# Expert stage of a two-model fp32 decoder kernel: extra places for weight chunks, filled at the stage's head

## What is computed

```python
h = h + hybrid_mixer(rms_norm(h, attn_norm[l]), ...)                     # model 1
h = h + hierarchical_moe(rms_norm(h, ffn_norm[l]), ...)
# model 2
x = x + gate1 * mixer(modulate(rms_norm(x, norm1_g), shift1, scale1))
x = x + gate2 * hier_moe(modulate(rms_norm(x, norm2_g), shift2, scale2), ...)
# every expert, for the tokens sent to it:
y = (silu(xb @ w_gate[e]) * (xb @ w_up[e])) @ w_down[e]
```

## Time and profile before

| | us |
|---|---|
| median of 3 runs | 2646.03 (2636.53 to 2647.21) |
| profiled execution, its time | 2646.7 |
| its span in the trace | 2644.5 |
| TensorE matmul busy | 2110.3 (80%) |
| VectorE busy | 631.6 (24%) |
| ScalarE busy | 361.4 (14%) |
| GpSimd busy | 59.7 (2%) |
| HBM read | 776.75 MB, 294 GB/s over the span |

### The profile page before, as it was taken

How to read it: one execution, slowest core, us unless ns; L and a number is a source line. 1 busy time by engine, 2 the same in 40 slices (tenths; PEclk the granted TensorE clock), 3 DMA queues, 4 the chain that set the end, 5 groups by cost and what they waited for, 6 DMA issues and landing times. The chain is left out here.

```text
span 2644.5 us, 33419 instructions
## 1 busy us (share of the span) xinstructions
PE 2110.3 (80%) x14160; PEld 1308.1 (49%) x14161; DVE 631.6 (24%) x1396; ACT 361.4 (14%) x733; POOL 59.7 (2%) x96
## 2 busy tenths in 40 slices
PE   7888779888777999899766666789999987666665
PEld 5564336564333688788422222238887862222222
DVE  4451104551012244453200000022441120000001
ACT  1520001520002131101100000011211020000000
POOL 0200000200000000000000000000000000000000
PEclk9999899999887999799888878799989988888888
DMA  9239999237998341386699999973302339999997
GB/s 385 120 145 427 428 428 399 95 139 309 429 428 357 112 159 66 129 344 239 273 428 429 428 428 429 428 291 128 132 31 96 127 128 423 427 429 428 429 428 306
DMA packets 55840, 779.33 MB, mean 295 GB/s; under 512 B 6840, under 2 KB 7096, under 8 KB 8120
## 3 DMA queue, kind: packets, MB, share of 16 engines
q1 hardware_dynamic: 55736, 777.82, 70.8%
HBM read 776.75 MB, written 1.05 MB: 294 GB/s over the span
## 5 line engine op out<-in xcount | busy, mean ns | idle before, releaser
L1899 PE MATMUL bank<-ring,arena 128*32 128x512 f32 x3136 | 505.5, 782 | 338.3 <-DMA ring<-in_w_exp 334.7
L1899 PEld LDWEIGHTS bank<-ring,arena 128*32 128x32 f32 x3136 | 102.2, 127 | 729.5 <-DMA ring<-in_w_exp 494.3
L1924 PE MATMUL bank<-ring,arena 128*32 128x512 f32 x1568 | 192.0, 628 | 66.5 <-DMA ring<-in_w_exp 43.8
L960 PE MATMUL bank<-xnT,ring 128*128 128x256 f32 x960 | 210.7, 379 | 0.0
L2079 DVE TENSOR_TENSOR arena<-bank,arena 128x256 f32<-128x256 f32 (+1 forms) x33 | 18.3, 554 | 795.7 <-PE bank L1899 566.4
L960 PEld LDWEIGHTS bank<-xnT,ring 128*128 128x128 f32 x960 | 181.6, 190 | 28.4 <-issue 4.5
L1636 PE MATMUL bank<-xnT,ring 128*128 128x256 f32 x768 | 177.2, 385 | 10.3 <-PEq L838 10.3
L1636 PEld LDWEIGHTS bank<-xnT,ring 128*128 128x128 f32 x768 | 148.3, 193 | 32.6 <-issue 11.9
L1869 PE MATMUL bank<-arena 128*128 128x256 f32 x592 | 144.6, 399 | 3.6 <-DVE arena L2090 3.6
L1869 PEld LDWEIGHTS bank<-arena 128*128 128x128 f32 x592 | 114.7, 200 | 65.0 <-issue 49.9
L1924 PEld LDWEIGHTS bank<-ring,arena 128*32 128x32 f32 x1568 | 50.2, 112 | 180.5 <-issue 95.2
(11 more groups left out here) (376 smaller groups left out, 2041.0 us busy)
## 6 DMA issues: line engine op xcount, KB each, us to landing
ring<-in_w_exp SPq DMA_DIRECT2D x288, 2048.0 KB, 25.7
arena<-in_w_ada SPq DMA_DIRECT2D x24, 2048.0 KB, 12.0
ring<-in_w_in SPq DMA_DIRECT2D x20, 2048.0 KB, 25.7
ring<-in_w_merge SPq DMA_DIRECT2D x18, 2048.0 KB, 7.9
ring<-in_w_o SPq DMA_DIRECT2D x8, 2048.0 KB, 10.3
ring<-in_w_conv SPq DMA_DIRECT2D x6, 2048.0 KB, 8.0
ring<-in_w_rest SPq DMA_DIRECT2D x2, 1696.0 KB, 25.5
small<-in_small SPq DMA_DIRECT2D x2, 1440.0 KB
```

The costliest lines, as they stand in the source:

```text
L960: last = nc.tensor.matmul(o[:, T * j:T * j + T], w[:, k, col:col + P], xnT[:, k, :], start=k == 0, stop=k == KT - 1)
L1899: last = nc.tensor.matmul(o[rows(e), :], Xw[:, k, rows(e)], ring[:, slot(n), at:at + MW], start=k == 0, stop=k == KT - 1)
L1924: last = nc.tensor.matmul(o[rows(e), :], hidT[:, j, rows(e)], ring[:, slot(n), at:at + MW], start=j == 0, stop=j == ft - 1)
```

## The change

Chunks that the ring has no slot for get places of their own in the arena, and are loaded during the head.

- `Xw` and `Yw` move from the arena into `xnT`; the rest of the stage's buffers move together, and the small scratch of e2's head moves into `small`. That leaves room for three chunks, `extra[0]` to `extra[2]`.
- e1 (`EXTRA1 = 2`): chunks 0 and 1 of quad 1 are loaded into `extra` at the head. GpSimd waits until the last item of quad 0 has used ring slots 0 and 1, and copies the two chunks there (128x4096 each), adding 16 to `w_loaded` as a load would. SyncE fetches quad 1 from chunk 2 on.
- e2 (`EXTRA2 = 3`): chunks 0 to 2 of quad 0 are loaded into `extra` at the head; the ring holds chunks 3 to 8 in place of 0 to 5. TensorE reads the first three from `extra` in item 0 and doesn't count them in `w_used`; SyncE fetches 9 to 11 as the ring frees.
- `extra[1]` overlies the scratch of the norm, so that its load waits for `scaled`. GpSimd's clearing of `Yw`, now in `xnT`, waits until the tokens are turned.

```diff
 RET, RWKV, LORA, CONV, MERGE, OUT2, MOE2 = 0, 4, 7, 8, 11, 20, 22
+EXTRA1, EXTRA2 = 2, 3
 ADA_CHUNKS, ADA_P1, ADA_HEADS = 12, 4, 2
...
             else:
-                load(sp, n, dram["w_exp2"][l, n - MOE2])
+                load(sp, n, dram["w_exp2"][l, n - MOE2 + EXTRA2])
...
         xtok = ar(0, TT, D)
-        Xw = ar(2048, KT, P)
-        silu, hid = ar(3072, F2), ar(3584, F2)
-        hidT = ar(4096, F2 // P, P)
-        Yw = ar(4608, D)
-        onehot, gw = ar(5632, TT, P), ar(5888, TT, P)
-        gwT = ar(6144, T)
-        rank_tab = ar(6400, ROUNDS * NE * TT)
-        gate_tab = ar(6912, (NQ + 1) * QUAD * TT)
+        Xw = xnT[:, 0:4, :].rearrange("p a (b s) -> p (a b) s", s=P)
+        Yw = xnT[:, 4:8, :].rearrange("p a t -> p (a t)")
+        silu, hid = ar(2048, F2), ar(2560, F2)
+        hidT = ar(3072, F2 // P, P)
+        onehot, gw = ar(3584, TT, P), ar(3840, TT, P)
+        gwT = ar(4096, T)
+        rank_tab = ar(4352, ROUNDS * NE * TT)
+        gate_tab = ar(4864, (NQ + 1) * QUAD * TT)
+        extra = [ar(5632 + SLOT * i, SLOT) for i in range(3)]
         RANK_AT, GATE_AT, LOADS_AT, QUAD_AT, LAST_AT = (i * (ITEMS + 1) for i in range(5))
...
                 sem(f"{tag}_{n}") for n in ("onehot", "xlow", "xhigh", "xlowtaken", "xhightaken", "silu", "hid", "hidturned", "hidT", "gw", "gwturned", "gwT", "y1", "y1taken", "y0taken", "sum"))
-            at = 13572
+            at = 13824
+            extra_in = sem(f"{tag}_extra")
+            extras = EXTRA1 if shared else EXTRA2
+            held = 0 if shared else EXTRA2
+
+            def ar(o, *shape, n=P):
+                size = int(np.prod(shape))
+                v = (arena[0:n, o:o + size] if shared else small[0:n, o - at + SMALL2:o - at + SMALL2 + size])
+                if len(shape) == 2:
+                    v = v.rearrange("p (a b) -> p a b", a=shape[0])
+                return v
+
             lg = ar(at, TT, nr)
...
-                    for n in range(RING, per_turn):
+                    for i in range(extras):
+                        e = (0, 2, 1)[i] if not shared else i
+                        if e == 1:
+                            sp.wait_ge(scaled, KT)
+                        sp.dma_start(extra[e], feed(1, e) if shared else feed(0, e)).then_inc(extra_in, 16)
+                    for n in range(RING + held, per_turn):
                         sp.wait_ge(w_used(), n0 + n - RING + 1)
...
                             last_item = sp.value_load(offs[0:1, LAST_AT + q - 1:LAST_AT + q], min_val=0, max_val=ITEMS * per_turn)
-                            for n in range(RING):
+                            for n in range(EXTRA1 if q == 1 else 0, RING):
                                 sp.wait_ge(w_used(), last_item + (n0 + n + 1))
...
                         def here(n):
+                            if first_item and n < held:
+                                pe.wait_ge(extra_in, 16 * extras)
+                                return extra[n]
                             pe.wait_ge(w_loaded(slot(n)), loads + 16 * ((n0 + n) // RING + 1))
+                            return ring[:, slot(n), :]
...
                                 if k % 2 == 0:
-                                    here(n)
+                                    w = here(n)
                                 for e in range(QUAD):
                                     at = MW * (QUAD * (k % 2) + e)
-                                    last = nc.tensor.matmul(o[rows(e), :], Xw[:, k, rows(e)], ring[:, slot(n), at:at + MW], start=k == 0, stop=k == KT - 1)
-                                if k % 2:
+                                    last = nc.tensor.matmul(o[rows(e), :], Xw[:, k, rows(e)], w[:, at:at + MW], start=k == 0, stop=k == KT - 1)
+                                if k % 2 and not (first_item and n < held):
                                     last.then_inc(w_used(), 1)
...
                     nc.gpsimd.memset(gwT, 0.0)
+                    pool.wait_ge(tok_turned, 2 * TT)
                     nc.gpsimd.memset(Yw, 0.0).then_inc(gwT_ready, 1)
+                    if shared:
+                        pool.wait_ge(tables_ready, 1)
+                        last_item = pool.value_load(offs[0:1, LAST_AT:LAST_AT + 1], min_val=0, max_val=ITEMS * per_turn)
+                        for n in range(EXTRA1):
+                            pool.wait_ge(extra_in, 16 * extras)
+                            pool.wait_ge(w_used(), last_item + (n0 + n + 1))
+                            nc.gpsimd.tensor_copy(ring[:, slot(n), :], extra[n]).then_inc(w_loaded(slot(n)), 16)
...
                 project_out2(l)
-                moe("e2", lambda q, n: dram["w_exp2"][l, q * 12 + n], MOE2, F2, wr2, NG2, row[0:1, 0:R2_N], gains[:, 1, :], mod[:, 24:32], mod[:, 40:48], (2, l + 1) if l + 1 < L else None)
+                moe("e2", lambda q, n: dram["w_exp2"][l, q * 12 + n], MOE2 - EXTRA2, F2, wr2, NG2, row[0:1, 0:R2_N], gains[:, 1, :], mod[:, 24:32], mod[:, 40:48], (2, l + 1) if l + 1 < L else None)
                 next_layer()
```

## The result

The changed kernel took **2630.48 us** in the median of 9 runs (2625.27 to 2636.45), beside 2646.03 us in 9 runs of the kernel before (2636.53 to 2649.3): a ratio of 0.9946, with an interval of 0.9934 to 0.9958. The forecast was 2618 us, with a range of 2607 to 2630. So the sign was right, and about half of the expected 28 us is missing. The profiled execution spans 2629.2 us, where before's spans 2644.5. A ratio here is the one on record for the runs of both kernels; it can differ from the quotient of their medians by up to 0.0017. One run of all those in this document (2668.98 us, of b1_e1_late) was a slow one, at a granted clock of 0.856 in place of 0.903, and the ratios leave it out.

The account below looks back on a forecast made before the run. The prediction took the stream of chunks, 4.895 us each, as the bound. From the profiled 2646.7 us it took 9.4, 9.4, 5.1 and 4.1, giving 2618.7; with that execution 0.7 above the median, it forecast 2618 us, range 2607 to 2630.

Parts of the forecast that it names:

- What bounds the kernel: Expert stages: from the first item on, the gapless stream of chunks binds, 4.895 us a chunk, not TensorE.
- e2, 9.4 us each: Each e2 stage: three chunks leave the stream, which starts 5.25 us later; gain 9.4 us.
- e1, 5.1 and 4.1 us: First and second e1 stage: two chunks leave the stream, which runs dry before chunk 4; gains 5.1 and 4.1 us.
- The copies, 3.8 us each and hidden: e1: GpSimd's two chunk copies take 3.8 us each and end before item 1 wants them, costing nothing.
- the held VectorE: Rival, e1: copies hold up VectorE through shared ports; 2628 to 2633 us where e1's gain is lost; chance 0.12.
- the slow copy: Rival, e1: slow copies delay item 1; over 13 us slower (2662 us) at about 25 us a copy; chance 0.04.
- Behind a stage the gain is kept: After each expert stage: the next stage's loads lie in the same stream, so no gain is lost there.
- The clock rival: Rival, expert stages: TensorE, waiting less, is granted a lower clock and eats the head start; 2640 to 2650 us; chance 0.06.
- The chances: Whole kernel: forecast 0.72, rivals 0.06, 0.12, 0.06 and 0.04; faster 0.88, within 0.5% 0.08, slower 0.04.
- e1 being lost: Both e1 stages: their gain lost and paid for ends at 2633 us, from which the range's top of 2630 was taken.

Follow-up runs that it names:

- b1_e1_late: a1_order with e1's two extra chunks being 4 and 5 of quad 1 instead of 0 and 1: 2608.87 us, 0.9857 of the kernel before.
- a1_order: The changed kernel with the next layer's early loads, at the end of the first e2 stage, in order of use: 2623.1 us, 0.9904 of the kernel before.
- c1_before_order: The kernel before with only the next layer's early loads, at the end of the first e2 stage, put in order of use: 2645.9 us, 0.9996.
- c2_copy_three: a1_order with each GpSimd chunk copy in e1 made three times in a row: 2617.64 us, 0.9884 of the kernel before.
- b3_both_late: a1_order with extra chunks 4 and 5 of quad 1 in e1 and 8 to 10 of quad 0 in e2: 2598.24 us, 0.9811 of the kernel before.

## Why the prediction was wrong in its size

- **What bounds the kernel: right.** The stream of chunks, 4.895 us each before and 4.897 after; TensorE's busy time didn't move.
- **e2, 9.4 us each: right.** 9.6 and 9.8 (9.1 to 11.4 over all traces with the same three chunks). First issue 7.13 us behind the first matmul (7.2), and the extra chunks were in time.
- **e1, 5.1 and 4.1 us: right.** 5.6 and 3.1 in after, 4.5 and 4.0 in a1_order (4.5 to 5.8 and 2.8 to 4.2 over all traces with the same two chunks). The stream does run dry (a DMA share of 0.86 there); b1_e1_late, where it doesn't, gets 9.8 and 8.7.
- **The copies, 3.8 us each and hidden: right.** 3.57 us; made three times each, 10.7 us, they cost nothing that shows, which also settles the rivals of the held VectorE and of the slow copy, up to that length.
- **"Behind a stage the gain is kept": this step failed.** I read it from the stage behind e1, where TensorE had no wait for a load, and took the same for e2. There the change moves n0 from 22 to 19, and with it the order of the early loads. I had costed n0 as a number of chunks, and it is also the rotation of the ring. The price was there to be worked out: six chunks of 4.895 us from the last expert chunk are 29.4 us, while the way from that chunk to the first projection before is 1745.75 - 1729.21 = 16.5 us, so 12.8 us late. Measured: 13.5 us after, 13.4 in before with the same order. With it the sum would have been about 2631 us, and the measured median is 2630.48. That the two agree to a microsecond is luck too, given the chance of several microseconds outside the stages.
- **The clock rival:** in the last long stretch the granted clock reads 0.82 after and 0.85 before, with the stream as full as ever. This isn't the fall that the rival supposed: over the same 2212 to 2590 us it is 0.84 in before, 0.81 in after, and also 0.81 in c1_before_order, whose work and whose stream are those of before. And it cost nothing, since the chunks came every 4.897 us.
- **The chances:** no case said "one stage's gain is paid back behind it". The range's upper end of 2630 came from e1 being lost; the true cause was a different one that came, by luck, to nearly the same time, half a microsecond outside the range.

## What to carry to other kernels

Where loads run through a ring, a change to how many chunks pass through it turns the ring for everything behind: write out, for each next consumer, in which order its chunks are issued and which of them it wants first, and price the one that moves back at chunks times the stream's pace, less the time by which it used to be early. Of chunks loaded ahead into extra places, choose those whose turn comes last in the window, so that the first freed slot still starts the stream at once; here that made 9.6 us a stage of e2 into 14 to 15.7. And one stage without a wait shows nothing about another stage that ends by the same code with another number.

## What the runs showed of the hardware

- GpSimd's copy of 128x4096 fp32 takes 3.60 us, 0.88 ns an element, and two in a row take 7.14. This is less than the clearing of 1024 elements in the earlier trace rows suggested (0.93 ns).
- A VectorE instruction of 0.43 us with both inputs in SBUF lasts until 0.27 us behind the end of a copy that runs beside it (up to 3.77 us in c2_copy_three; 0.76 and 0.94 us in b1_e1_late and 1.14 in b3_both_late, whose late copies meet L2035 and L2048, their makers of the next one-hot); one with an input in PSUM doesn't. A copy can be the one that is longer: in the second e1 stage of c2_copy_three L2039 starts at 624.41, 0.08 us ahead of a copy, and takes its 0.42 us, while the copy takes 3.81 instead of 3.60.
- The last `combine` took 3.69 us in before and in four other traces, and 5.3 to 6.1 us in the remaining seven, among them that of c1_before_order, which does the work of before. The row of it in the timeline of before, of after and of c1_before_order, in this order:

```profile
2628.17 3.69 PE L1869 MATMUL bank<-arena 128*128 128x256 f32 x16 [0.91 <-DVE arena L2090]
```

```profile
2610.75 5.84 PE L1887 MATMUL bank<-arena,xnT 128*128 128x256 f32 x16 [0.89 <-DVE xnT L2120]
```

```profile
2626.62 5.99 PE L1874 MATMUL bank<-arena 128*128 128x256 f32 x16 [0.89 <-DVE arena L2095]
```

  The combine accounts for 2.2 of the 2.9 us at the end of the table. The granted clock over the last 25 us is 0.84 in before and 0.73 in c1_before_order, so the same 16 matmuls fell more at the lower of TensorE's two levels (1.2 GHz). I take it for chance of the execution, since c1_before_order has it without a change of work; which executions get it was not tried.
- Executions of the same work differ by up to 4.8 us in the time up to the first expert stage (-4.2 to +0.6 in the table). A single trace's total can't weigh a change of that size. Differences within one trace, stage by stage, can weigh one of about 1.5 us in the first three expert stages, and one of about 2 us in the last.
